# A decoder layer on one core: the three matmul passes of a weight chunk over 256, 272 and 264 columns instead of 264 each

## The reference, cut to what matters

```
proj = rmsnorm(x, g_mix_pre) @ w_in            # 2048 x 7184, split among three groups of heads
A: HGRN2 recurrence (4 heads); B: gated DeltaNet (8 heads, causal conv of width 4); C: RG-LRU (512 channels)
x  = x + rmsnorm(concat(oa, ob, oc) @ w_out, g_mix_post)        # 2048 x 2048
h2 = rmsnorm(x, g_ffn_pre)
x  = x + rmsnorm((silu(h2 @ w_gate) * (h2 @ w_up)) @ w_down, g_ffn_post)   # 5632 wide
```

## Time and profile before

| | |
|---|---|
| time, median of 3 runs | 1513.33 us (1513.06 to 1514.56) |
| profiled execution, first to last instruction | 1510.1 us |
| the rest of the time, by the median | 3.2 us |
| PE busy | 1437.4 us, 95% |
| DVE busy | 850.4 us, 56% |
| ACT busy | 663.0 us, 44% |
| POOL busy | 166.8 us, 11% |
| DMA | 233.96 MB, mean 155 GB/s |

### The profile page before, as it was taken

The page is one execution under the profiler, slowest core; times in us unless marked ns, Lnnn a source line. Parts: engine busy times, 40 slices in busy tenths (PEclk is TensorE's granted clock), DMA queues, the critical chain, the costliest instruction groups (busy, mean ns, idle before and its releaser), DMA issues.

```text
span 1510.1 us, 28509 instructions
## 1 busy us (share of the span) xinstructions
PE 1437.4 (95%) x11533; PEld 1415.0 (94%) x11533; DVE 850.4 (56%) x1119; ACT 663.0 (44%) x843; POOL 166.8 (11%) x196
## 2 busy tenths in 40 slices
PE   6999999999997989896999999999999999999996
PEld 5998999999997989896999999999999999999996
DVE  5756665665466695656655555555555554443444
ACT  6543534435363446544644444444444443343333
POOL 4022232223222200021000000000000000000001
PEclk9999999999998999998999999999999999999998
DMA  6442533425353544453555555555555555555551
GB/s 205 147 140 84 174 94 111 145 83 159 88 177 101 158 126 144 141 185 96 170 181 181 180 180 181 179 181 179 182 180 180 181 181 181 182 183 159 181 178 58
DMA packets 225166, 233.96 MB, mean 155 GB/s; under 512 B 10459, under 2 KB 220414, under 8 KB 224820
## 3 DMA queue, kind: packets, MB, share of 16 engines
q1 hardware_dynamic: 220420, 218.86, 47.0%
q0 software_dynamic: 4672, 14.04, 2.8%
HBM read 223.45 MB, written 9.65 MB: 154 GB/s over the span
## 4 chain that ended last, share of the span: by engine, by line
PE 84%; DVE 8%; ACT 4%; issue 2%; POOL 1%; DVEq 0%; ACTq 0%; POOLq 0%
PE ps L605 24%; PE ps L606 24%; PE ps L607 24%; DVE conv L1544 1%; PE ps L752 1%; PE ps L746 1%; PE ps L718 1%; DVE w_lo L1424 1%; PE ps L755 1%; PE ps L765 1%; ACT w_hi L1021 1%; PE ps L627 1%; POOL Ss L523 1%; PE ps L851 1%; ACT L1021 1%
## 5 line engine op out<-in xcount | busy, mean ns | idle before, releaser
L1424 DVE TENSOR_TENSOR w_lo<-raw,w_hi 128x1024 fp32r<-128x1024 f32 x408 | 500.7, 1229 | 495.2 <-ACT w_hi L1021 494.2
L1021 ACT ACTIVATE w_hi<-raw 128x1024 fp32r<-128x1024 f32 x408 | 431.5, 1058 | 657.5 <-PE ps L607 657.3
L605 PE MATMUL ps<-act_hi,w_hi 128*128 128x264 f32 x2304 | 674.0, 293 | 13.7 <-issue 11.0
L606 PE MATMUL ps<-act_lo,w_hi 128*128 128x264 f32 x2304 | 659.5, 286 | 0.0
L607 PE MATMUL ps<-act_hi,w_lo 128*128 128x264 f32 x2304 | 658.8, 286 | 0.0
L605 PEld LDWEIGHTS ps<-act_hi,w_hi 128*128 128x128 f32 x2304 | 439.9, 191 | 15.7 <-issue 12.4
L606 PEld LDWEIGHTS ps<-act_lo,w_hi 128*128 128x128 f32 x2304 | 440.6, 191 | 0.4
L607 PEld LDWEIGHTS ps<-act_hi,w_lo 128*128 128x128 f32 x2304 | 438.9, 190 | 0.0
L605 PE MATMUL ps<-hid_hi,w_hi 128*128 128x264 f32 x704 | 200.8, 285 | 2.4 <-issue 2.4
L606 PE MATMUL ps<-hid_lo,w_hi 128*128 128x264 f32 x704 | 200.9, 285 | 0.0
L607 PE MATMUL ps<-hid_hi,w_lo 128*128 128x264 f32 x704 | 200.6, 285 | 0.0
(11 more groups left out here) (307 smaller groups left out, 1325.9 us busy)
## 6 DMA issues: line engine op xcount, KB each, us to landing
raw<-in_w_in_dram SPq DMA_DIRECT2D x112, 512.0 KB, 3.6
raw<-in_w_gate_dram SPq DMA_DIRECT2D x88, 512.0 KB, 3.5
raw<-in_w_up_dram SPq DMA_DIRECT2D x88, 512.0 KB, 3.5
raw<-in_w_down_dram SPq DMA_DIRECT2D x88, 512.0 KB, 3.4
raw<-in_w_out_dram SPq DMA_DIRECT2D x32, 512.0 KB, 3.4
out_dram<-Ss POOLq DMA_DIRECT2D x12, 512.0 KB, 3.8
Ss<-in_state_gdn_dram POOLq DMA_DIRECT2D x8, 512.0 KB, 6.1
xtok<-in_x_prompt_dram SPq DMA_DIRECT2D x2, 1024.0 KB, 5.9
```

The costliest lines, as they stand in the source:

```text
L605: pe.matmul(out, wh, x_hi[:, kk], start=(kk == begin), stop=False)
L606: pe.matmul(out, wh, x_lo[:, kk], start=False, stop=False)
L1021: return act.activation(out, in_, f, **kw)
L1424: tt(w_lo[:, slot], raw[:, slot], w_hi[:, slot].bitcast(F32), sub).then_inc(lo_done, 1)
```

## The change: what it does

The buffers of x_lo grow from 264 to W = 272 columns. Their first eight hold a copy of the sample's x_hi, made on VectorE by `sample_copy`, and the 264 of x_lo follow. The three passes become: w_hi on the 256 prompt columns of x_hi, w_hi on all 272 columns of the new x_lo buffer, and w_lo on the 264 of x_hi. So the sample's high product lands in columns 0 to 7 of the bank, its two other products in columns 264 to 271, and the prompt's sums in 8 to 263. `join` on VectorE copies the eight columns of both banks out to `first8` and adds them to the last eight; every reader of a group now waits for `joined` in place of `pe_used`. There are 88 joins. The results move by eight columns in their bank. To find room, the gate matrix for c_wa moves into the place of `QK`, and its clearing and loading move from the kernel's start to the stretch between the B and A heads on GpSimd's queue.

```
-                        out = ps[:, 2 * par + m, 0:T]
-                        pe.matmul(out, wh, x_hi[:, kk], start=(kk == begin), stop=False)
-                        pe.matmul(out, wh, x_lo[:, kk], start=False, stop=False)
-                        last = pe.matmul(out, wl, x_hi[:, kk], start=False, stop=(kk == nk - 1))
+                        out = ps[:, 2 * par + m]
+                        pe.matmul(out[:, NB:T], wh, x_hi[:, kk, 0:L], start=(kk == begin), stop=False,
+                                  skip_group_check=True)
+                        pe.matmul(out[:, 0:W], wh, x_lo[:, kk], start=False, stop=False,
+                                  skip_group_check=True)
+                        last = pe.matmul(out[:, NB:W], wl, x_hi[:, kk], start=False, stop=(kk == nk - 1),
+                                         skip_group_check=True)
...
             def acc_ready(g):
-                act.wait_ge(pe_used, 4 * g + 4)
+                act.wait_ge(joined, g + 1)
...
+            def sample_copy(hi, lo_):
+                dve.tensor_copy(lo_[:, :, 0:NB], hi[:, :, L:T])
+
+            def join(g, par, used):
+                dve.wait_ge(pe_used, used)
+                dve.tensor_copy(first8[:, :, :], ps[:, 2 * par:2 * par + 2, 0:NB]).then_inc(half_in, 1)
+                dve.wait_ge(half_in, g + 1)
+                last8 = ps[:, 2 * par:2 * par + 2, T:W]
+                tt(last8, last8, first8[:, :, :], add).then_inc(joined, 1)
...
             def round_(r, kind, mixer, fin, before=lambda pos: None):
                 for pos in range(SLOTS):
                     lo(SLOTS * r + pos + AHEAD, (pos + AHEAD) % RING)
                     q = pos // 4
+                    if pos in (4, 8, 12):
+                        join(4 * r + q - 1, (q - 1) % 2, SLOTS * r + pos)
+                    if pos == 0 and not first:
+                        join(4 * r - 1, 1, SLOTS * r)
                     before(pos)
...
             for pos in range(4 * OUT_GROUPS):
                 lo(OUT_C0 + pos + AHEAD, (pos + AHEAD) % RING)
+                if pos == 0:
+                    join(27, 1, OUT_C0)
+                if pos == 7:
+                    join(OUT_G0, 0, OUT_C0 + 7)
...
             b_mixer(3)
+            gate_blocks(0, c_wa)
             a_mixer(4, 0)
```

More of the change, by code:

```diff
@@ L34 @@
 T = L + NB
+W = T + NB
 D = 2048
@@ L109, in hybrid_layer @@
         rbc = put("rbc", [P, T])
+        first8 = put("first8", [P, 2, NB])
         ident = masks[:, 0, :]
@@ L115, in hybrid_layer @@
         cat_hi = put("cat_hi", [P, KT, T], F32R)
-        cat_lo = put("cat_lo", [P, KT, T], F32R)
+        cat_lo = put("cat_lo", [P, KT, W], F32R)
         qkv = put("qkv", [P, 4, 2, T])
@@ L166, in hybrid_layer @@
         cm = put("cm", [P, 4, T], offset=place["decay"] + 8 * 4 * T)
-        wbd = put("wbd", [P, 2, 4, P])
+        wbd = [put("wbd_a", [P, 4, P], offset=place["QK"]), put("wbd_x", [P, 4, P])]
         xtok = [put("xtok0", [P, D], offset=place["kb"]), put("xtok1", [P, D], offset=place["sq"]),
@@ L213, in hybrid_layer @@
         drained = [sem("drained0"), sem("drained1")]
+        joined = sem("joined"); half_in = sem("half_in")
         g_done = sem("g_done")
@@ L664, in gate_columns @@
                     pe.matmul(out, gw_hi[:, k], act_hi[:, k], start=(k == 0), stop=False)
-                    pe.matmul(out, gw_hi[:, k], act_lo[:, k], start=False, stop=False)
+                    pe.matmul(out, gw_hi[:, k], act_lo[:, k, NB:W], start=False, stop=False)
                     last = pe.matmul(out, gw_lo[:, k], act_hi[:, k], start=False, stop=(k == KT - 1))
@@ L923, in gate_products @@
                 for t in range(4):
-                    last = pe.matmul(ps[:, 4 + t, 0:T], wbd[:, w, t, :], qkv[:, t // 2, t % 2, :], start=True, stop=True)
+                    last = pe.matmul(ps[:, 4 + t, 0:T], wbd[w][:, t, :], qkv[:, t // 2, t % 2, :], start=True, stop=True)
                 return last
@@ L1284, in _, with out_evac @@
             round_(6, "c", True, lambda pos: a_step(pos, 5, 1))
-            def out_evac(k, par, n, c_ready, gain, dst):
-                act.wait_ge(pe_used, c_ready)
+            def out_evac(k, par, n, g_ready, gain, dst):
+                act.wait_ge(joined, g_ready)
                 if k >= 3:
@@ L1301, in out_evac @@
                     tile = 2 * k + t
-                    last = A(dst[:, tile], ps[:, 2 * par + t, 0:T], scale=params[:, gain + tile:gain + tile + 1])
+                    last = A(dst[:, tile], ps[:, 2 * par + t, NB:W], scale=params[:, gain + tile:gain + tile + 1])
                     if t == 1:
@@ L1648, in finish @@
                 dve.wait_ge(mx["ohi"], n + 1)
-                tt(cat_lo[:, ds(tile0, 2)], oT[:, :, :], cat_hi[:, ds(tile0, 2)].bitcast(F32), sub)\
+                sample_copy(cat_hi[:, ds(tile0, 2)], cat_lo[:, ds(tile0, 2)])
+                tt(cat_lo[:, ds(tile0, 2), NB:W], oT[:, :, :], cat_hi[:, ds(tile0, 2)].bitcast(F32), sub)\
                     .then_inc(mx["olo"], 1)
@@ L1718, in round_ @@
             def round_(r, kind, mixer, fin, before=lambda pos: None):
+                first = isinstance(r, int) and r == 0
                 for pos in range(SLOTS):
@@ L1795, in rg_step @@
                     dve.wait_ge(c_["hi"], 1)
-                    tt(cat_lo[:, 12:16], cm[:, :, :], cat_hi[:, 12:16].bitcast(F32), sub).then_inc(c_["lo"], 1)
+                    sample_copy(cat_hi[:, 12:16], cat_lo[:, 12:16])
+                    tt(cat_lo[:, 12:16, NB:W], cm[:, :, :], cat_hi[:, 12:16].bitcast(F32), sub)\
+                        .then_inc(c_["lo"], 1)
                 if pos == 6:
@@ L1802, in _ @@
                 lo(OUT_C0 + pos + AHEAD, (pos + AHEAD) % RING)
+                if pos == 0:
+                    join(27, 1, OUT_C0)
+                if pos == 7:
+                    join(OUT_G0, 0, OUT_C0 + 7)
+                elif pos > 7 and pos % 4 == 0:
+                    join(OUT_G0 + pos // 4 - 1, (pos // 4 - 1) % 2, OUT_C0 + pos)
                 rg_step(pos)
@@ L1823, in input_lo @@
                 dve.wait_ge(nz_hi, 1 + q)
+                sample_copy(act_hi[:, 4 * q:4 * q + 4], act_lo[:, 4 * q:4 * q + 4])
                 for k in range(4 * q, 4 * q + 4):
-                    last = stt(act_lo[:, k], xT[:, k], params[:, G_FFN_PRE + k:G_FFN_PRE + k + 1],
+                    last = stt(act_lo[:, k, NB:W], xT[:, k], params[:, G_FFN_PRE + k:G_FFN_PRE + k + 1],
                                act_hi[:, k].bitcast(F32), mul, sub)
                 last.then_inc(nz_lo, 1)
+            join(OUT_G0 + OUT_GROUPS - 1, 1, FF_C0)
             add_squares(0, OUT_GROUPS - 1)
@@ L1847, in gate_scale @@
             def gate_scale(g):
-                dve.wait_ge(pe_used, 8 * g + FF_C0 + 4)
+                join(2 * g + FF_G0, 0, 8 * g + FF_C0 + 4)
                 if not isinstance(g, int) or g > 0:
                     dve.wait_ge(drained[1], g + FF_G0 // 2)
+                dve.wait_ge(joined, 2 * g + FF_G0 + 1)
                 tt(sgate[:, :, :], acc(0), rbc[:, :].unsqueeze(1).broadcast_to([P, 2, T]), mul).then_inc(drained[0], 1)
@@ L1861, in up_evac @@
                 dve.wait_ge(gate_r, g + 1)
-                dve.wait_ge(pe_used, 8 * g + FF_C0 + 8)
+                join(2 * g + FF_G0 + 1, 1, 8 * g + FF_C0 + 8)
                 if not isinstance(g, int) or g > 0:
                     dve.wait_ge(nz_lo, g + 4)
+                dve.wait_ge(joined, 2 * g + FF_G0 + 2)
                 tt(hidF[:, :, :], sgate[:, :, :], acc(1), mul).then_inc(drained[1], 1)
@@ L1906, in _ @@
                 g, i = divmod(c - AHEAD, DOWN_CH)
+                if i == 0 and g:
+                    join(DOWN_G0 + g - 1, (g - 1) % 2, DOWN_C0 + DOWN_CH * g)
                 if i == 1 and g > 1:
                     add_squares(1, g - 1)
+            join(DOWN_G0 + DOWN_GROUPS - 1, 1, CHUNKS)
             add_squares(1, DOWN_GROUPS - 1)
```

37 lines of the change are left out of this document (21 added, 16 removed).

## The result

| | before | after |
|---|---|---|
| median, 4 runs of each on one chip | 1513.19 us | 1526.75 us (1525.66 to 1527.89) |
| ratio, 95% interval | | 1.0097 (1.0082 to 1.0111) |
| profiled execution, first to last instruction | 1510.1 us | 1524.2 us |

The prediction said 1528 with 1500 to 1537 as its range. The profiled execution of the changed kernel has a time of its own, 1525.66 us; 1.5 us of it lie outside the span, and so it is in every later run. So of the 3.2 us that the prediction put outside the span of the kernel before, about 1.7 were something else: its profiled execution was that much quicker than its median. By the spans the change costs 14.1 us, against 15.2 in the forecast's sum.

A forecast was written before the change was run, and what follows sets the result against it. It took TensorE, busy 95% of the span, as the bound. Passes 0 plus join delays of 15.2 us on the 1513.3 us median gave 1528.5 us; the range meant to hold 8 in 10 was 1500 to 1537.

The forecast's parts named there:

- the rival that fell: All chunks: the 256-column pass is cheaper than the straight line, 26 us less, 1505.5 us in all; chance 0.31.
- Passes, 0: All chunks: column cost is a straight line, so a triple of matmuls stays at 363.3 ns; 0 us.
- the third rival: All chunks: the tiles' new places cost pace, 1.4 ns a matmul, 13.7 us on top, 1542 us; chance 0.08.
- Position 4, 1.2 a round: Rounds 1 to 3: ScalarE's read-out waits for the join behind `lo`, delaying `convolve`; 1.2 us each round.
- Position 8, 1.2 a round: Rounds 1 to 3: `convolve` again starts later, where TensorE waits for VectorE already; 1.2 us each round.
- Rounds 4 and 5, start: Late read-outs in round 4 cost 0.2 us, round 5 nothing; round 0 and sixteen `sample_copy` at the start 0.9.
- Round 6, 2.4: Round 6: late ScalarE copies for line 833 at position 4, 1.2 us, and late `convolve` at position 8, 1.2.
- a rival with 0.04: GpSimd's scaling is let through early, shrinking TensorE's 9.6 us wait by up to 7; 1521 us, chance 0.04.
- Head, 1.8: Output projection: the first ScalarE read-out, heading the RG-LRU chain, waits for the join behind `lo`; 1.8 us.
- First read-out 1.1: Output projection: the first group's read-out starts after its join, so TensorE enters the bank later; 1.1 us.
- Norm and first gate and up 0.9: A norm's unhidden first read-out, 0.4 us, and `sample_copy` ahead of the first gate and up tiles, 0.5.
- Gate matrix, 0: GpSimd's moved clearing and loading, about 2 us, falls under its 6.1 us wait for the stores; 0 us.

The follow-up runs named there:

- the joins first: Changed kernel with each join of the rounds and output projection ahead of VectorE's `lo` instead of behind it; 1517.01 us, ratio 1.0038.
- the shifted one: Kernel before the change with 64 unused bytes behind `rbc`, so all tiles behind it lie 64 bytes further; 1514.35 us, ratio 1.0011.
- the passes alone: Changed kernel without any join, readers waiting for TensorE alone and the sample's high-by-high product left out; 1518.21 us, ratio 1.0036.

## Why the prediction was right, and where it was not

Its time was right to 2 us and its main mechanism is shown, by the joins first: read-outs that queue behind `lo`. That the sum came so near is in part luck: of its 15.2 us several terms missed, in both directions, and position 8 and rounds 4 and 5, over by 3.2 and 2.2, with 1.3 at the start and the step of half clock in round 3 (1.6), stand against 1.2 at position 4, 1.4 in round 6, 1.5 at the head, 1.7 in gate and up and 1.1 at the end. Two slips of the sum itself are small: 363.3 less 355 is 8.3 and not 8.1 (27 us instead of 26, in the rival that fell), and 22 us of delays give 1535 and not 1537.

- **Passes, 0.** The price of a column was right: 117.8 ns forecast for pass one, 117.6 measured; it is a line of 0.447 ns a column, inside 0.42 to 0.46. Wrong was "a triple stays 363.3": the tile's new rows add 1.25 ns, 1.7 us in gate and up, and 0.7 to 0.9 in down. That is the third rival in small: 0.4 ns a matmul. It stood in the prediction with 1.4 ns a matmul, from a comparison of down with gate, and 0.08. That comparison was too large, as the window over down holds a break of TensorE of 2.4 us and a stretch of half clock; in groups without either a triple of down took 365.1 ns before, 0.6 ns a matmul above gate.
- **Position 4, 1.2 a round.** Measured 2.0 (3.6 less a stretch of half clock; 2.1 from chunk 16 to 24), 1.25 and 1.6: too small by 0.4 in the mean.
- **Position 8, 1.2 a round.** The step that failed: 0.1 to 0.2. The prediction took the wait at 746 as proof that TensorE stands right behind `convolve`, and did not ask what `convolve` itself was waiting for.
- **Rounds 4 and 5, start.** 0.2 and 0.9 forecast; -2.0 and -0.4 measured. Of the 2.0, 1.6 are the clock, and the rest moves in kernels without joins too (the shifted one, with the same stretch gone, has -2.4 and -0.4).
- **Round 6, 2.4.** 3.8 measured, by a mechanism that the prediction had as a rival with 0.04 and priced as a gain: the order at what GpSimd and VectorE share. Its trigger was none of the joins but 64 bytes. With the order kept, the forecast delays cost 2.3, and one more stretch of half clock 1.7.
- **Head, 1.8.** 2.85 at once and 0.4 behind. The missing 1.3 us are ScalarE's table load, which used to run in the shadow ahead of the read-out; the prediction moved a wait and did not list what else stands behind it. First read-out 1.1: measured 1.0. Norm and first gate and up 0.9: measured 1.3, against 0.7 with the passes alone.
- **Gate matrix, 0; joins in gate and up, 0.** Shown both: the run without the loading, and 1.68 us in that stretch with joins and without.

## What to carry to other kernels

A small operation costs by its place in the queue: put it where its engine waits anyway, ahead of the long independent one, and list all that stands behind a new wait, table loads too. Where two delays lie over each other, halves don't add up, and removing one shows nothing in the time: read both by stretches, against the same work's start, and read the clock's record of each stretch before explaining 1.6 us of it. Adding a tile moves the others; here one that large transfers read was better at a multiple of 256 bytes than 64 bytes behind one, the only two places tried.

## What the runs showed of the hardware

Stores of 512 KB from a tile that starts 64 bytes past a multiple of 256 land in 5.0 to 5.1 us (medians), from one at a multiple in 3.7 to 3.8. Of the loads into it the four of rounds 5 and 6 take 5.0 to 5.6 at a multiple and 5.8 to 6.3 shifted; the other eight show no clear step (5.6 to 6.3 and 5.8 to 6.9).

An fp32r matmul costs 3.5 ns and 0.447 ns a column, by the line through 256 and 512 columns, which 288, 320 and 384 meet within 1 ns. The place and the distance of the rows that it reads move a triple by 1.3 to 2.1 ns.

GpSimd's scaling of Ss takes 3.6 to 3.7 us (round 6 with Ss at a multiple of 256) or 7.6 to 11.4 (every other one in rounds 5 and 6): the short ones start beside VectorE's scans, which then take 4.76 us instead of 1.37, the long ones beside its short two-input operations. What in these operations does it wasn't tried. Two VectorE operations of `convolve`, 0.76 us together, took 3.86 beside it. The Trainium skill, "SBUF — State Buffer", section SBUF: two separate sides, describes a lock between the two engines that is held for a whole instruction. The 3.86 us agree with it; that VectorE's two-input operations kept their 0.42 us while GpSimd's one operation stretched to 11.43 doesn't fit "the other fully blocks" as it stands.
